# Weight tiles in pairs at both turns of a long convolution, and a branch product one tile ahead of its lower part

## What is computed

```python
proj = h @ w_in                                  # hyena part, q, k, v, gates
z = parts[0]
for n in range(HYENA_ORDER):                     # 2 long convolutions
    z = parts[n + 1] * fftconv(z, hk[:, n], dbias[n])
y_hy = z @ w_hy_up
o = diff_attention(q, k_all, v_all, lam)
y_att = heads_out(o, subln_g, lam_init) @ w_att_up
mixed = (g_hy * y_hy + g_att * y_att) @ w_out    # g_*: sigmoid gates
x = x + g1 * rmsnorm_2(mixed, g_mix_post)
x = x + g2 * rmsnorm_2(swiglu(...), g_ffn_post)
```

## Time and profile before

| | us |
|---|---|
| median of 3 runs | 3357.23 |
| lowest, highest | 3356.16, 3363.36 |
| the profiled execution | 3355.29 |
| its span in the trace | 3353.5 |
| TensorE busy in it | 3125.0 |
| VectorE, ScalarE, GpSimd busy | 1637.9, 1010.8, 426.5 |

### The profile page before, as it was taken

One profiled execution on the slowest core, in us unless ns is written; L12 is line 12 of the kernel. 1 busy time (PEld: TensorE's weight loads), 2 busy tenths in 40 slices (PEclk: granted clock), 3 DMA queues, 4 the chain that ended last, 5 costly groups with the idle time before them and its releaser, 6 DMA issues.

```text
span 3353.5 us, 33558 instructions
## 1 busy us (share of the span) xinstructions
PE 3125.0 (93%) x13822; PEld 2514.2 (75%) x13822; DVE 1637.9 (49%) x1752; ACT 1010.8 (30%) x1203; POOL 426.5 (13%) x177
## 2 busy tenths in 40 slices
PE   6898878999999999989999998889988999999996
PEld 2683557778888888778888876777767788888885
DVE  3777665566556564574521055577435422222225
ACT  2344445242222221233321123467222221111111
POOL 0396760000000000000200033100010000000000
PEclk8998887899999999989999999999998999999998
DMA  5113442223223222221332243442321112111112
GB/s 203 44 45 106 142 147 79 72 87 102 77 74 126 96 94 81 101 76 63 123 121 102 94 151 132 110 99 53 110 95 71 68 48 63 41 44 63 32 51 107
DMA packets 96193, 301.24 MB, mean 90 GB/s; under 512 B 11206, under 2 KB 15046, under 8 KB 95848
## 3 DMA queue, kind: packets, MB, share of 16 engines
q1 hardware_dynamic: 96040, 299.09, 27.3%
HBM read 251.34 MB, written 47.71 MB: 89 GB/s over the span
## 4 chain that ended last, share of the span: by engine, by line
PE 81%; DVE 9%; ACT 3%; issue 3%; DMA 2%; POOL 1%; SPq 0%; DVEq 0%; ACTq 0%; POOLq 0%
PE ps L705 67%; PE ps L751 3%; PE ps L766 2%; PE ps L1093 2%; PE ps L1118 2%; PE ps L808 1%; DVE ps L1990 1%; PE ps L1103 1%; DVE tmp L1864 1%; PE ps L793 1%; DVE mainf L1857 1%; DMA mainr<-sc_k 1%; DVE tmp L2264 1%; DVE mainr L1871 1%; DVE tmp L2258 1%
## 5 line engine op out<-in xcount | busy, mean ns | idle before, releaser
L705 PE MATMUL ps<-mainr,wh 128*128 128x512 f32 (+1 forms) x7104 | 1943.4, 391 | 42.5 <-POOL wl L2415 11.5
L705 PEld LDWEIGHTS ps<-mainr,wh 128*128 128x128 f32 x7104 | 1335.6, 189 | 322.5 <-issue 46.0
L705 PE MATMUL ps<-mainr,wl 128*128 128x512 f32 (+1 forms) x3552 | 1130.9, 389 | 0.0
L705 PEld LDWEIGHTS ps<-mainr,wl 128*128 128x128 f32 x3552 | 671.7, 189 | 139.1
L1214 ACT CAST wh<-raw 128x1024 fp32r<-128x1024 f32 (+2 forms) x320 | 281.8, 886 | 726.5 <-PE ps L705 549.5
L1688 DVE TENSOR_TENSOR wl<-raw,wh 128x1024 fp32r<-128x1024 f32 (+2 forms) x256 | 248.0, 970 | 465.5 <-ACT wh L1214 465.4
L2415 POOL TENSOR_TENSOR wl<-raw,wh 128x1024 fp32r<-128x1024 f32 x64 | 154.4, 2419 | 454.5 <-ACT wh L1214 454.5
L751 PE MATMUL ps<-mainr,wh 128*128 128x512 f32 x576 | 167.2, 414 | 40.8 <-issue 27.4
L1947 DVE TENSOR_TENSOR mainf<-mainf,ps 128x1024 f32<-128x1024 f32 x80 | 97.6, 1220 | 215.1 <-PE ps L705 215.1
L1990 DVE SCALAR_TENSOR_TENSOR ps<-mainf,vec,ps 128x1024 f32<-128x1024 f32 (+1 forms) x174 | 180.9, 1102 | 0.8 <-ACT ps L1403 0.7
L2453 POOL TENSOR_TENSOR tmp<-tmp,mainf 128x1024 f32<-128x1024 f32 x8 | 27.5, 3442 | 1179.2 <-DMA mainf<-in_rope 1117.3
(11 more groups left out here) (228 smaller groups left out, 2583.9 us busy)
## 6 DMA issues: line engine op xcount, KB each, us to landing
raw<-in_mod_w SPq DMA_DIRECT2D x48, 512.0 KB, 4.5
raw<-in_ada_w SPq DMA_DIRECT2D x48, 512.0 KB, 3.6
raw<-in_f_up SPq DMA_DIRECT2D x44, 512.0 KB, 4.2
raw<-in_g_up SPq DMA_DIRECT2D x44, 512.0 KB, 3.5
raw<-in_w_in SPq DMA_DIRECT2D x40, 512.0 KB, 4.1
raw<-in_pw SPq DMA_DIRECT2D x24, 512.0 KB, 3.6
sc_x<-mainf SPq DMA_DIRECT2D x24, 512.0 KB, 2.6
mainf<-sc_x SPq DMA_DIRECT2D x24, 512.0 KB, 6.1
```

The source lines that it names most:

```text
L705: ins = e.matmul(out, wt[:, a:b], xs[n], start=kk == 0 and t == 0, stop=kk == kt - 1 and t == 2)
```

## The change

On TensorE the first two forward tiles of each order are made side by side: for each `kk`, 6 matmuls of tile 0 and then 6 of tile 1. So are the two weights of the first inverse tile: for each of the eight Z tiles, 3 matmuls with b = 0 and 3 with b = 1. All other tiles stay as they were. In the forward turns ScalarE, VectorE and GpSimd make a weight's halves one tile further ahead (+4), and so do ScalarE and VectorE in `att_up`. There VectorE's order is new: product of tile i, lower part of tile i-1, weight halves of tile i+3.

```diff
+    def three(j, a, hi, lo, out, first, last):
+        for t, (wt, x) in enumerate(((k.WH(j), hi), (k.WH(j), lo), (k.WL(j), hi))):
+            ins = e.matmul(out, wt[:, a:a + 128], x, start=first and t == 0, stop=last and t == 2)
+        return ins
+
+    def forward(o, fts):
+
+        for kk in range(4):
+            for event in [("foldhi", 3), ("foldlo", 3)] if o == 0 else [("pmhi", kk), ("pmlo", kk)]:
+                w.wait_ge(*k.at(*event))
+            for ft in fts:
+                j = k.W["dft", o, ft]
+                if kk == 0:
+                    hold_weight(j)
+                    hold_acc("dft", o, ft)
+                for ab in range(2):
...
+                if kk == 3:
+                    ins.then_inc(*k.to("tile", j))
+
+    def backward(o, tt, parts):
+
+        for ft in range(8):
+            for event in ("zhi", o, ft), ("zlo", o, ft):
+                w.wait_ge(*k.at(*event))
+            for b in parts:
+                j = k.W["idft", o, tt, b]
+                if ft == 0:
+                    hold_weight(j)
...
     for o in range(2):
-        for ft in range(8):
...
+        for fts in [(0, 1)] + [(ft,) for ft in range(2, 8)]:
+            forward(o, fts)
         for tt in range(4):
             hold_acc("idft", o, tt)
...
+            for parts in [(0, 1)] if tt == 0 else [(0,), (1,)]:
+                backward(o, tt, parts)
@@ -1556,7 +1580,7 @@
         for ft in range(8):
-            split_to(k.W["dft", o, ft] + 3)
+            split_to(k.W["dft", o, ft] + 4)
@@ -1657,7 +1681,7 @@
     for i in range(ND):
-        split_to(k.W["att_up", i] + 3)
+        split_to(k.W["att_up", i] + 4)
@@ -2380,15 +2404,19 @@
-    for i in range(ND):
-        t = k.TMP("mg", i, 1)
-        split_to(k.W["att_up", i] + 3)
-        w.wait_ge(*k.at("tile", k.W["att_up", i]))
-        w.wait_ge(*k.at("gl1", i))
-        e.tensor_tensor(t, k.ACC("att_up", i), t, ALU.mult).then_inc(*k.to("mg", i, 1))
-        w.wait_ge(*k.at("mghi", i))
-        w.wait_ge(*k.at("mgadd", i))
-        e.tensor_tensor(k.R(20 + i), t, k.R(k.MIX(i)).bitcast(F32), ALU.subtract).then_inc(*k.to("mglo", i))
+    for i in range(ND + 1):
+        if i < ND:
+            t = k.TMP("mg", i, 1)
+            w.wait_ge(*k.at("tile", k.W["att_up", i]))
+            w.wait_ge(*k.at("gl1", i))
+            e.tensor_tensor(t, k.ACC("att_up", i), t, ALU.mult).then_inc(*k.to("mg", i, 1))
+        if i:
+            t = k.TMP("mg", i - 1, 1)
+            w.wait_ge(*k.at("mghi", i - 1))
+            w.wait_ge(*k.at("mgadd", i - 1))
+            e.tensor_tensor(k.R(19 + i), t, k.R(k.MIX(i - 1)).bitcast(F32), ALU.subtract).then_inc(*k.to("mglo", i - 1))
+        if i < ND:
+            split_to(k.W["att_up", i] + 4)
```

More of the change, by code:

```diff
@@ L1047, in tensor_program @@
             turn_context(23)
-    for o in range(2):
-        for ft in range(8):
-            j = k.W["dft", o, ft]
-            hold_weight(j)
-            hold_acc("dft", o, ft)
-            for ab in range(2):
-                src = ab if ft in EVEN else 1 - ab
-                ins = product(j, 4, lambda kk: ([k.PM(0)[:, src, kk, :]], [k.PM(1)[:, src, kk, :]]),
-                              lambda kk: [("foldhi", 3), ("foldlo", 3)] if o == 0 else [("pmhi", kk), ("pmlo", kk)],
-                              [k.ACC("dft", o, ft)[:, 512 * ab:512 * ab + 512]], 512 * ab)
-            ins.then_inc(*k.to("tile", j))
+    def three(j, a, hi, lo, out, first, last):
+        for t, (wt, x) in enumerate(((k.WH(j), hi), (k.WH(j), lo), (k.WL(j), hi))):
+            ins = e.matmul(out, wt[:, a:a + 128], x, start=first and t == 0, stop=last and t == 2)
+        return ins
@@ new lines, in forward @@
+    def forward(o, fts):
[8 more added lines that the diff above has]
+                for ab in range(2):
+                    src = ab if ft in EVEN else 1 - ab
+                    ins = three(j, 512 * ab + 128 * kk, k.PM(0)[:, src, kk, :], k.PM(1)[:, src, kk, :],
+                                k.ACC("dft", o, ft)[:, 512 * ab:512 * ab + 512], kk == 0, kk == 3)
+                if kk == 3:
+                    ins.then_inc(*k.to("tile", j))
@@ new lines, in backward @@
+    def backward(o, tt, parts):
[6 more added lines that the diff above has]
+                    hold_weight(j)
+                part = b if ft in EVEN else 1 - b
+                ins = three(j, 128 * ft, k.Z(0)[:, part, ft, :], k.Z(1)[:, part, ft, :],
+                            k.ACC("idft", o, tt)[:, 512 * b:512 * b + 512], ft == 0, ft == 7)
+                if ft == 7:
+                    ins.then_inc(*k.to("tile", j))
@@ L1061, in tensor_program @@
+    for o in range(2):
+        for fts in [(0, 1)] + [(ft,) for ft in range(2, 8)]:
+            forward(o, fts)
         for tt in range(4):
             hold_acc("idft", o, tt)
-            for b in range(2):
-                j = k.W["idft", o, tt, b]
-                part = lambda ft: (0 if ft in EVEN else 1) if b == 0 else (1 if ft in EVEN else 0)
-                hold_weight(j)
-                product(j, 8, lambda ft: ([k.Z(0)[:, part(ft), ft, :]], [k.Z(1)[:, part(ft), ft, :]]),
-                        lambda ft: [("zhi", o, ft), ("zlo", o, ft)],
-                        [k.ACC("idft", o, tt)[:, 512 * b:512 * b + 512]]).then_inc(*k.to("tile", j))
+            for parts in [(0, 1)] if tt == 0 else [(0,), (1,)]:
+                backward(o, tt, parts)
```

## The result

The changed kernel took 3335.64 us, the median of 4 runs (3334.69 to 3337.81); the kernel before, run 4 times beside it, 3359.41. The ratio is put at 0.9938, interval 0.9926 to 0.995: some 21 us faster (the two medians lie 23.8 us apart), where 28.7 were forecast. Executions of one kernel differ: 15 later ones of the kernel before took 3352.76 to 3359.9 us. The profiled execution took 3335.38 us with a span of 3333.6, 19.9 less than the span before.

The account below looks back on a forecast made before the run. TensorE, busy 93% of the span, was taken as the bound, so only its stalls counted. Turns 4.1 + 9.7 - 0.3 = 13.5 us plus branches 15.2 made 28.7: 3328.5 us, own range 3325 to 3331, wide range 3324 to 3336.

Parts of the forecast that it names:

- The first product: First forward turn: VectorE's first product starts near 1934.5 in the trace, 2.2 us later than before.
- The idle time before the first pair: First inverse turn: after 3 matmuls TensorE stands 3.6 us for the pair's second weight; the turn gains 4.1 us.
- the chain from D to the second weight: Turns: from the start of VectorE's first product (D) to the inverse pair's second weight being ready, 38.06 us.
- The clock loss behind the stall: First inverse turn: lower clock after the wait for the second weight costs 1.70 us, bounds nothing and 2.38.
- The forward pair in order 0: First forward turn: tile 0 ends 4.08 us later; a load hides half, so VectorE's first product is 2.2 us later.
- The second turn: Second order's turns: the 4.97 us stall and its clock loss go, one 3.6 us stall comes; gain 9.7 us.
- The transposes: Second order: ScalarE's weight cast, 1 us long, delays the copy TensorE's transposes wait for; loss 0.3 us.
- The branches: `att_up` to the start of w_out: weights split earlier, one 1.2 us stall left, no clock loss; gain 15.2 us.
- The rival with a late third weight: Start of w_out: third weight's raw tile loaded late, idle 5 us, 9.7 of 15.2 left, 3334.0 us; 12%.
- The attention: Stage after the turns: its start moves with the tiles ahead; no gain or loss of its own.
- The slow matmul pace of a pair: Paired matmuls: alternating weights and accumulators slows TensorE; gain gone from 0.15 us each, 3367 at lower clock; 3%.
- The cast not a period earlier: Turns: ScalarE's further-ahead weight cast comes no sooner, inverse pairs wait 5.9 us more each, 3341.7 us; 8%.

Follow-up runs that it names:

- run 4: Not a label: in "run 4 times" it counts the executions of the kernel before, measured beside the changed kernel, median 3359.41 us.
- The cut operation: Changed kernel with GpSimd's lower half of forward weight 3 cut in two, one half before and one behind VectorE's `hc` of tile 0, both orders: 3334.5 us, ratio 0.9928.
- branches alone: Kernel before with only the `att_up` part of the change, the turns left as they were: 3343.92 us, ratio 0.9962.
- the changed kernel's second trace: The changed kernel run once more, unaltered: 3335.93 us, ratio 0.9937.

## Why the prediction was right and wrong

- **The first product** was forecast 9.73 us behind the start of the turn and came at 9.72.
- **The idle time before the first pair**, forecast 3.6, was 4.47. This is the step that failed in the turns: the chain from D to the second weight was taken from rows in which GpSimd's operation lay in the slot of the two PSUM products. The splits four ahead put GpSimd's first one across `hc` of tile 0, 1.06 us. The cut operation gave the forecast's idle time back, 3.53. The clock loss behind the stall was 2.9 us, not 1.70, outside the bound of 2.38; other traces of the same turns had 2.2 to 2.9 there. First turn 1.9 instead of 4.1.
- **The forward pair in order 0** was kept at a price of 2.2 us on the first product. Without it the first product came 7.9 us behind the start, GpSimd's operation no longer covered `hc`, the stall was 1.68 us with no clock loss, and the turns' mark 4.8 us less: in order 0 it only cost.
- **The second turn**: no stall ahead, as forecast, the same 1.06 us, idle 4.46, clock loss 1.7 (1.4 to 3.0 in other traces). 8.7 instead of 9.7. The forecast's 36 matmuls for 9 ahead of the lower part counted the new order within a tile in: 9 of the 27 come from it, 18 from the pair.
- **The transposes**: 1.72 us of wait for 1.40, the 0.3 forecast.
- **The branches**: the lower part no longer waited and two of the stalls went, as forecast. The step that failed is the split's price: 1.22 us was taken from a row where GpSimd was idle; in the new order every split but the first lies beside GpSimd's sum, and the large ones take 3.35 to 3.42. Idle 3.38 us instead of 1.2, and 1.5 us of half clock instead of none: 11.4 instead of 15.2. The forecast's "no clock loss" held in three traces with the same stall (branches alone among them), and the changed kernel's second trace lost 2.8 us. The rival with a late third weight named the place and 9.7 us, but a late load as its cause; with the split moved off GpSimd the loads were in time.
- **The attention** was not in the sum. It was priced as moving with what stands ahead of it, at nothing of its own; it took 3.7 us more. Over all traces here it ranges from 212.7 to 217.2 us, and the kernel before had nearly the shortest form, so the range was some 4 us too narrow on the slow side. The cause of the 3.7 us stays open.
- **The slow matmul pace of a pair** did not show; pairs run at 0.227 us at full clock. **The cast not a period earlier** did not either.

Of the 8.8 us missing, 3.3 are the turns (2.1 of idle time from GpSimd beside VectorE, 1.2 of clock) and 3.8 the branches (some 2.2 and 1.5); 3.7 are the attention; 2.0 came back by chance. The median of 3335.64 us lies outside the forecast's own 3325 to 3331 and just inside the wide range up to 3336, which was widened for a late third weight: that it lies inside is luck.

The Trainium skill, SBUF — State Buffer, section Who interferes with whom, states the rule that the prediction should have weighed: a VectorE instruction with two SBUF inputs contends with a GpSimd instruction that reads SBUF, the shared pair of ports being an exclusive lock, and the order of issue decides who is blocked. The traces agree in each case here: 2.35 us for 1.29, 3.35 for 1.22, and no delay for the products out of PSUM.

## What to carry to other kernels

Before an instruction is moved, look at what the other engines run at its new place, not only at what waits for it: a duration holds for the neighbours it was measured with. If two instructions keep each other out, let the one that nobody waits for stand second, or cut it to the length of the slot. And before a difference of 1 to 4 us behind a stall or in an unchanged stage is put down to a change, look how far two traces of the same code lie apart there.

## What was not expected of the hardware

- VectorE and GpSimd shut each other out for whole instructions, in turns: GpSimd's sum took 3.25 to 3.31 us for 2.39 when VectorE's lower part had started first, and VectorE's split behind it 3.35 for 1.22.
- Equal stalls cost unequal stretches of lower clock. The stalls of 4.45 to 4.47 us before the second weight cost 1.4 to 3.0 us in the six traces of the changed turns (2.9 and 1.7 in the first); the stall of 3.38 us in w_out cost nothing in branches alone, 1.5 us in the changed kernel's first trace and 2.8 in its second; the pause of 2.5 us cost 1.7 us in that second trace and none in the first.
- An unchanged stage of 213 us had 216.45 and 216.49 us in two traces of one kernel, 214.1 and 214.4 in two kernels with the same code up to its end, and 212.7 to 217.2 over all, with the clock low at other places.
